# Expert passes of 32 slots in place of 64, with the products in quarters of the array's columns

## The reference, cut to what matters

```
(silu(x @ w_gate[e]) * (x @ w_up[e])) @ w_down[e]        # w_gate, w_up: 1024 x 512; w_down: 512 x 1024
y[token] += weight * that                                 # weight: the router's, two experts for each token
```

## Time and profile before

| | before |
|---|---|
| median of 3 runs | 1564.17 us (1560.15 to 1565.51) |
| span of the profiled execution | 1562.6 us |
| PE busy | 1474.9 us (94%) |
| DVE busy | 463.8 us (30%) |
| ACT busy | 233.9 us (15%) |
| bytes moved | 400.81 MB, mean 256 GB/s |

### The profile page before, as it was taken

The page is one execution under the profiler, slowest core; times in us unless marked ns, Lnnn a source line. Parts: engine busy times, 40 slices in busy tenths (PEclk is TensorE's granted clock), DMA queues, the critical chain, the costliest instruction groups (busy, mean ns, idle before and its releaser), DMA issues.

```text
span 1562.6 us, 21450 instructions
## 1 busy us (share of the span) xinstructions
PE 1474.9 (94%) x8392; PEld 946.4 (61%) x8393; DVE 463.8 (30%) x835; ACT 233.9 (15%) x469; POOL 22.0 (1%) x69
## 2 busy tenths in 40 slices
PE   5999999999989999999799999999989998999998
PEld 2866774544444444444485657777768564777775
DVE  1355545311111111111544321111145472111112
ACT  1230002200000000000313430000031062100001
POOL 2000000000000000000000000000000000000000
PEclk7999999999999999999999999999999999999999
DMA  9665524899999999999998150344276923144420
GB/s 376 226 247 216 217 109 170 344 424 421 423 385 399 425 428 426 425 428 424 407 405 323 51 219 22 142 160 161 81 285 249 395 93 108 54 162 161 161 81 27
DMA packets 89961, 400.81 MB, mean 256 GB/s; under 512 B 7040, under 2 KB 12288, under 8 KB 63264
## 3 DMA queue, kind: packets, MB, share of 16 engines
q1 hardware_dynamic: 89888, 399.73, 64.4%
HBM read 398.66 MB, written 1.05 MB: 256 GB/s over the span
## 4 chain that ended last, share of the span: by engine, by line
PE 75%; DMA 10%; DVE 7%; issue 3%; DVEq 3%; ACT 1%; SPq 0%; ACTq 0%
PE psum L1349 20%; PE psum L1019 12%; PE psum L1362 10%; DMA ring<-in_moe_up 7%; PE psum L1164 5%; PE psum L629 4%; PE psum L1312 4%; PE psum L1007 2%; DMA arena<-in_w_mod 2%; PE psum L752 2%; PE psum L566 2%; PE psum L1197 2%; PE psum L1182 1%; DMA ring<-in_ada_w 1%; DVE arena L1894 1%
## 5 line engine op out<-in xcount | busy, mean ns | idle before, releaser
L1019 PE MATMUL psum<-ring,arena 128*64 128x256 f32 (+1 forms) x2240 | 306.8, 428 | 20.8 <-DMA ring<-in_moe_up 8.7
L1349 PE MATMUL psum<-arena,ring 128*128 128x256 f32 x1408 | 313.3, 381 | 0.1
L1349 PEld LDWEIGHTS psum<-arena,ring 128*128 128x128 f32 x1408 | 268.8, 191 | 54.5 <-issue 19.5
L1019 PEld LDWEIGHTS psum<-ring,arena 128*64 128x64 f32 x2240 | 161.7, 138 | 174.3 <-issue 80.2
L1362 PE MATMUL psum<-ring,arena 128*128 128x512 f32 x352 | 157.9, 592 | 0.0
L2043 DVE TENSOR_SCALAR arena<-psum,cols 128x256 f32<-128x256 f32 x44 | 24.0, 544 | 325.5 <-PE psum L1349 325.5
L1164 PE MATMUL psum<-arena,ring 128*128 128x256 f32 x512 | 113.5, 383 | 0.2
L1164 PEld LDWEIGHTS psum<-arena,ring 128*128 128x128 f32 x512 | 97.8, 192 | 16.0 <-issue 2.7
L1362 PEld LDWEIGHTS psum<-ring,arena 128*128 128x128 f32 x352 | 66.9, 190 | 66.3 <-issue 63.6
L1807 DVE TENSOR_TENSOR arena<-psum,arena 128x256 f32<-128x256 f32 x32 | 13.6, 425 | 254.8 <-PE psum L1019 254.8
L2383 ACT ACTIVATE arena<-arena 128x256 f32<-128x256 f32 x44 | 18.3, 417 | 417.8 <-DVE arena L2049 417.8
(11 more groups left out here) (381 smaller groups left out, 1214.4 us busy)
## 6 DMA issues: line engine op xcount, KB each, us to landing
ring<-in_moe_gate SPq DMA_DIRECT2D x28, 2048.0 KB, 19.6
ring<-in_moe_up SPq DMA_DIRECT2D x28, 2048.0 KB, 18.0
ring<-in_moe_down SPq DMA_DIRECT2D x28, 2048.0 KB, 18.6
arena<-in_w_mod SPq DMA_DIRECT2D x32, 1024.0 KB, 9.8
ring<-in_ada_w SPq DMA_DIRECT2D x12, 2048.0 KB, 10.4
ring<-in_w_qkv SPq DMA_DIRECT2D x12, 2048.0 KB, 15.0
ring<-in_w_ffn_gate SPq DMA_DIRECT2D x10, 2048.0 KB, 7.7
ring<-in_w_ffn_up SPq DMA_DIRECT2D x10, 2048.0 KB, 12.4
```

Source lines behind the costliest of these rows:

```text
L1019: ins = mm(bank[b][o, 0:n], lhsT, w[:, half * n:(half + 1) * n], start=first, stop=last, tile_position=(0, 64 * half))
L1349: last = mm(b[:, k * TOK:(k + 1) * TOK], sl[k][2][:, c, j * P:(j + 1) * P], hTd[:, c, :], start=(c == 0), stop=(c == DC - 1))
```

## The change

`WIN` goes from 64 to 32. A pass takes 32 slots, `product` puts four stationary copies of 32 columns side by side, each with a quarter of the weight matrix's columns, `add_y` works in four row groups of 32 partitions (`add_part`), each into its own bank, and the transposes become four matmuls against reordered columns of the identity. The routing table gets eight possible passes for each expert (`NWIN`), for which DVE has three more small operations before `mtab`. An expert with more than 32 slots takes two passes.

```diff
-WIN = 64
+WIN = 32
+NQ = P // WIN
 SLOTS = 2 * TOK
+NWIN = TOK // WIN
...
+            def add_part(t, q, first=False, final=False):
+
+                hs = slice(WIN * q, WIN * q + WIN)
+                return mm(bank[4 + q][:, TOK * t:TOK * t + TOK], pwin[hs, t * P:(t + 1) * P], ym[hs, :],
+                          start=(first and t == 0), stop=final, skip_group_check=True, tile_position=(WIN * q, 0))
+
+            def add_y(t):
+
+                for q in range(NQ):
+                    last = add_part(t, q)
                 return last
...
                 def product(b, lhsT, w, n, first, last):
-                    for half in range(2):
-                        o = slice(64 * half, 64 * half + 64)
-                        ins = mm(bank[b][o, 0:n], lhsT, w[:, half * n:(half + 1) * n], start=first, stop=last,
-                                 tile_position=(0, 64 * half))
+                    for q in range(NQ):
+                        ins = mm(bank[b][WIN * q:WIN * q + WIN, 0:n], lhsT, w[:, q * n:(q + 1) * n], start=first, stop=last,
+                                 tile_position=(0, WIN * q))
                     return ins
...
-                        last = product(1 + k, xw[:, c, :], w(c), 256, c == 0, c == DC - 1)
+                        last = product(1 + k, xw[:, c, :], w(c), P, c == 0, c == DC - 1)
...
                 for j in range(2):
-                    last = nc.tensor.transpose(bank[1][:, TOK + j * P:TOK + (j + 1) * P],
-                                               actm.rearrange("p (q j) -> p j q", j=2)[:, j, :], ident[:, :])
+                    for half in range(2):
+                        o = TOK + 2 * WIN * j
+                        last = mm(bank[1][64 * half:64 * half + 64, o:o + 2 * WIN],
+                                  actm.rearrange("p (q j) -> p j q", j=2)[:, j, :],
+                                  ident[:, :].rearrange("p (h o t) -> p o h t", o=2, t=WIN)[:, half], start=True, stop=True,
+                                  tile_position=(0, 64 * half))
...
-                    last = product(3, actT[:, k % 2, 64 * (k // 2):64 * (k // 2) + 64], w(k), 512, k == 0, k == 3)
+                    last = product(3, actT[:, k % 2, WIN * (k // 2):WIN * (k // 2) + WIN], w(k), D // NQ, k == 0, k == 3)
...
-            for t in range(NT):
-                add_y(t, name="moe_done")
+            for n in range(2):
+                for t in range(NT):
+                    for q in (2 * n, 2 * n + 1):
+                        add_part(t, q, final=True).then_inc(S("moe_done"), 1)
...
-                    dve.wait_ge(S("moe_done"), 2 * t + n + 1)
-                    half_of(ysum, t, n, gate2b, 4)
+                    dve.wait_ge(S("moe_done"), 4 * n + 4)
+                    d(V.tensor_tensor(ysum[:, t, 512 * n:512 * n + 512].rearrange("p (b m) -> p b m", b=2),
+                                      psum[:, 4 + 2 * n:6 + 2 * n, TOK * t:TOK * t + TOK],
+                                      gate2b[:, 512 * n:512 * n + 512].rearrange("p (b m) -> p b m", b=2), ALU.mult))
```

More of the change, by code:

```diff
@@ L1000, in gathered @@
                 for t in range(NT):
[L1001 to L1010, removed]
+                    for q in range(NQ):
+                        add_part(t, q, first=True)
+            def add_part(t, q, first=False, final=False):
[5 more added lines that the diff above has]
+                    last = add_part(t, q)
                 return last
@@ L1056, in entry @@
                     return mtab[0:1, bass.ds(i * 2 + n, 1)] if e >= FIRST else mtab[0:1, n:n + 1]
-                extra = pe.value_load(entry(NE + e), min_val=0, max_val=3)
+                extra = pe.value_load(entry(NE + e), min_val=0, max_val=NWIN - 1)
                 before = pe.value_load(entry(2 * NE + e), min_val=1, max_val=4 * NE)
@@ L1819, in _ @@
                 start = dve.value_load(mtab[0:1, bass.ds(i, 1)], min_val=0, max_val=SLOTS)
-                extra = dve.value_load(mtab[0:1, bass.ds(i + NE, 1)], min_val=0, max_val=3)
+                extra = dve.value_load(mtab[0:1, bass.ds(i + NE, 1)], min_val=0, max_val=NWIN - 1)
                 before = dve.value_load(mtab[0:1, bass.ds(i + 2 * NE, 1)], min_val=1, max_val=4 * NE)
@@ L2245, in pass_ @@
                 act.wait_ge(S("y_added"), done)
-                A(ym, bank[3][:, :], ACT.Copy).then_inc(S("ym_ready"), 1)
+                A(ym, bank[3][:, 0:D // NQ], ACT.Copy).then_inc(S("ym_ready"), 1)
             with act.Fori(0, NE, 1) as i:
-                extra = act.value_load(mtab[0:1, bass.ds(i + NE, 1)], min_val=0, max_val=3)
+                extra = act.value_load(mtab[0:1, bass.ds(i + NE, 1)], min_val=0, max_val=NWIN - 1)
                 before = act.value_load(mtab[0:1, bass.ds(i + 2 * NE, 1)], min_val=1, max_val=4 * NE)
```

48 lines of the change are left out of this document (28 added, 20 removed).

## The result

The changed kernel takes 1606.44 us (median of 4 runs, 1604.03 to 1611.18); the kernel before took 1563.87 in the same series (1560.15 to 1565.51). The ratio is 1.027, 95% interval 1.0244 to 1.0297: 42 us slower, where 1561.2 us and no visible difference were forecast.

What follows compares the result with a forecast made beforehand. DMA was taken to bound the kernel, with PE close behind. Landing -0.9, stage end -3.0 and clock +0.9 gave -3.0 us: 1559.6 us of span, 1561.2 us with the 1.6 us to the median; range 1556 to 1573.

Steps and rivals of the forecast that it cites:

- The frame: Expert stage: DMA alone sets when the last weights land, by total bytes plus every moment it had nothing to do.
- The products: Gate and up on PE: 128 matmuls of 128 columns, four abreast, take 4.0 us in place of 7.13.
- Rival 3: Gate and up instructions stay at 56 ns, a pass at 13.5 us: 1590 us, chance 0.09.
- The start: First experts: first load of expert 3 issued near 307.6 us; DVE's three added table operations cost nothing.
- Code: PE's instruction fetches and branch over the extra pass: 0.7 us for about 34 fetches' bytes, 1.0 for branch misses.
- Rival 2: Doubled experts with branch misses or loop-entry stalls at experts 0 to 5 starve DMA: 1572 us, chance 0.17.
- signs of being wrong: Passes over 11 us, L1084 long more than three times before expert 6, or fetches putting PE behind 14.8 us.
- Extra passes: Experts 0, 2 and 4 take a second pass of 7.7 us; DMA's first rest is 12.1 us, not 6.1.
- the walk: Load-queue calculation of DMA's rests: 12.5 us together against 15.1 before, so the last weights land 2.6 us earlier.
- The end of the stage: After the last weights: DVE takes the sum out 3.6 us earlier, with the gain limited to 3.0 us.
- the clock: PE's idle pieces bring a half clock, hidden in the DMA-bound part; 0.9 us charged at the stage's end.
- a cap: End of the expert stage: the slice L566, waiting for its load behind the experts', limits the gain to 3.0 us.

Runs made afterwards that it cites:

- experiment 1: Changed kernel with PE's branch and written-out extra pass only for experts 0, 2 and 4: 1564.40 us, ratio 0.999.
- experiment 7: Changed kernel without branch, extra-pass code or extra passes; slots beyond 32 of experts 0, 2 and 4 left out: 1553.44 us, ratio 0.9937.
- 3: Kernel before with a second, never executed copy of the pass behind the same branch, 92 matmuls to skip in place of 46: 1612.19 us, ratio 1.0292.
- 5: Changed kernel with the loads of experts 3 to 31 cut to an eighth of each row, PE's code unchanged: 1489.87 us, ratio 0.9526.
- experiment 9: Kernel before with the branch and its 46 unexecuted matmuls a second time, behind each expert's last pass: 1589.34 us, ratio 1.0154.
- 11: Changed kernel with only experts 0 to 5 written out and 6 to 31 in the loop of two: 1593.60 us, ratio 1.0185.
- Experiment 4: Kernel before without the branch and the written-out extra pass, valid only while no expert has over 64 slots: 1559.96 us, ratio 0.9965.
- experiment 2: Changed kernel with the pass written once, in a loop over extra + 1 without a branch, slots freed behind the loop: 1568.24 us, ratio 1.001.
- experiment 8: Kernel before (64 slots) with one written-out pass in a loop over extra + 1, slots freed after a wait for down_done: 1654.42 us, ratio 1.0529.

## Why the prediction was wrong, step by step

**The frame held.** "The time at which the last weights land is set by DMA alone" is the table above. From 550 to 780 us the share is 1.01 and the products wait for loads, as forecast.

**The products held.** 4.0 us were taken, 31 ns for each instruction; 3.70 us were measured, 29 ns, next to the 3.6 us by columns alone (28 ns for each of 128, where the prediction has 27). The figure of the Trainium skill for hardware decode off, some 62 ns of sequencer for each MATMUL ("TensorE: Matmul & The Clock Gate", section "Wait — 56ns, not 53.3ns?"), does not apply here: 29 ns is less than half of it. The 25 ns worked out from the 60 cycles of the Trainium skill's "TensorEngine Tiling (Array Packing)", Instruction Overhead, an estimate, are near. Rival 3 is out. The down product took 1.93 (1.9 forecast), the pass 9.31 (9.7), the extra pass, from expert 0's first down product at 306.24 to its second at 313.28, 7.0 us (7.7).

**The start held.** This execution was 2.3 us late before the experts began, as a load issue shows that the change does not touch (first row; the second is the load of expert 3 that waits for the first freed slot):

```profile
235.71 0.34 SPq L340 DMA_DIRECT2D ring<-in_moe_up  x1
...
310.20 0.33 SPq L340 DMA_DIRECT2D ring<-in_moe_gate  x1
```

The kernel before:

```profile
233.41 0.34 SPq L335 DMA_DIRECT2D ring<-in_moe_up  x1
```

Less these 2.3 us, expert 3's load is issued at 307.9; 307.6 was forecast. The gate product of expert 0 is 2.2 us later than before, so DVE's three added operations cost nothing, as said.

**The step that failed is "Code".** The prediction gave the branch 1.0 us and the fetched bytes 0.7; the two measure 42 us together (experiment 1 against the changed kernel). The number of fetches was right (about 34 were forecast for the first twelve experts; the trace has 35 from 295 to 508 us, where the thirteenth begins), and their bytes are small. What was wrong is the wait for them:

- The branch missed at eleven of the first fourteen experts, where "it may miss more" was priced at a few of experts 1 to 5.
- A miss took 3.5 to 6.9 us, where the earlier trace rows had 4.4 and 5.2, and 12 us of waits within the products came on top, which had no term at all.
- Each long one brought the half clock over the product behind it, 2.85 us, which I had called hidden in this part and charged only at the stage's end.
- Most of all, I reasoned that from expert 10 on a late branch falls while four loads are on their way. That is true of one branch, not when every expert takes 17.4 us against DMA's 14.77.

**Rival 2** had the mechanism, but ended it at expert 5 and at 1572 us, with a chance of 0.17. Of the prediction's own signs of being wrong, one showed: an expert took 17.4 us, over 11. The one for this cause, L1084 long more than three times before expert 6, did not: it was long three times there (experts 1, 3 and 5). The eight after that did most of the damage, and no step had priced them.

**Extra passes** cost 8 to 11 us without the code cost (experiment 7 against 1), where the walk gave about 7. With the skipped code gone (experiment 1) the kernel is at 1564.40 us, 3.2 above the forecast; this may be a part of it. It would not have changed the verdict.

**The end of the stage held in size, not in its path.** PE begins on the last up matrix at 738.28 before and at 783.65 after, 45.4 us later. The next stage's first product begins at 766.30 before (L1164) and at 808.58 after (L1177), 42.3 us later. So the end of the stage won 3.1 us; forecast were 3.0, less 0.9 for the clock. First PE's timeline after, then pieces of the chain that ended last:

```profile
783.65 3.59 PE L1026 MATMUL psum<-ring,arena 128*32 128x128 f32 x64 [2.25 <-DMA ring<-in_moe_up]
...
788.85 1.93 PE L1026 MATMUL psum<-ring,arena 128*32 128x256 f32 x32
791.29 1.16 PE L1012 MATMUL psum<-arena 32*128 32x256 f32 x16 [0.50 <-ACT arena L2266]
794.89 3.59 PE L571 MATMUL psum<-ring,small 128*1 128x512 f32 x16 [2.43 <-DMA ring<-in_w_mod]
```

```profile
792.60 0.70 DVE arena L1858
...
808.58 20.96 PE psum L1177 x96
```

The slice L571 waits for its load, as said, and runs at the half clock: 3.59 us, twice, where the earlier trace rows has 1.90. But it caps nothing: the chain from the sum to L1177 goes through DVE and ACT in both kernels and not through the slice. DVE takes the sum out 792.60 - 783.65 = 8.95 us after the up product begins, where it was 750.05 - 738.28 = 11.77. These 2.8 us are nearly the whole gain; 3.6 were forecast for this path, and the up product's half clock (3.59 us in place of some 1.85) took from it. That the sum came near 3.0 by way of a cap that did not bind is luck.

**What is shown and what is open.** Shown: the unexecuted code behind the branch is the whole loss (1, 3); it costs less with short loads (5), with short skips (9) and where the code is executed again soon (11, the loop). Shown too, by times alone: each long branch ends 1.3 to 1.5 us after a 16 KB packet of the fetch queue, and from 550 to 750 us, where no branch is long, the queue moves none. That PE resumes because the packet has come is the only reading that I see of it. Open: what starts a fetch, and how much code stays; the loop of two experts, with four written-out passes of 92 matmuls, did stay.

None of the experiments gives a kernel that takes every input and beats the one before. Experiment 4 is 0.35% faster but does not take an expert with over 64 slots, experiment 7 leaves slots out, and experiment 1, which fits these inputs alone, and experiment 2 only tie. A shorter pass on PE gives nothing while DMA moves the same bytes.

## What to carry to other kernels

Count the instructions that a branch skips, not only those that run: straight-line code that is executed once, with a skipped copy behind each part, can make an engine wait several us at a branch, and doubling the instructions of both made eleven long branches of two here. In a trace look at the durations of the branches and at idle time with the releaser "issue"; keep the rare path out of straight-line code, or write it into a loop, where it is executed or skipped again from code that is already there. And where one resource sets the time, compare the bytes that it moved in the same stretch of two kernels: here that one subtraction found the place and the size of the loss.

## What the runs showed of the hardware

- A branch over 92 unexecuted matmuls takes 3.3 to 3.8 us with the DMA engines at a share of 0.2 (experts 6 to 13), 3.5 us with them at 0.02, and 5.9 to 6.9 us with them at 0.95 or more at the same experts. The same branch takes 0.2 us once the loop's code has been executed, and 72 to 88 ns where PE goes on into the extra pass. Over 46 matmuls it is mostly 0.33 us, but 4.4 and 5.2 us in two cases of the kernel before, and 1.5 to 5.1 us in ten of fourteen when each expert has three written-out passes in place of two (experiment 9).
- A branch that is over 1 us long ends 1.3 to 1.5 us after the end of a 16 KB packet of the fetch queue: 49 of 49 in nine kernels. At experts 6 to 13 the packet starts 0.9 to 1.5 us after the branch with short loads, and with full ones 3.6 to 4.5 us after it in seven of eight cases; behind the doubled experts 0, 2 and 4 it is 1.6 to 2.1 us with full loads.
- Code arrives in packets of 16 KB during the execution, 41 of them from 290 to 550 us in the changed kernel. "Trainium Architecture — The Big Picture" of the Trainium skill (The software stack) has the instruction streams moved into the engines' instruction memory when the program is loaded; in this trace a part of them comes while it runs.
- Four matmuls of 32 columns side by side, 128 rows each and 128 columns long, run every 29 ns (128 in 3.70 us).
- Idle pieces of 2.3 to 2.9 us behind every expert brought the clock down for a part of the product behind them: granted 0.52 from 600.3 to 603 us and 0.95 from 603 to 611 (8.7 us in place of 7.13, so some 3.2 us at the half clock, experiment 8).
